# Expert loop: VectorE computes the rest of the U block ahead of the dot products of the fetched rows

## The reference

```python
def expert_block(args):
    hb, eb, gb = args
    a = jnp.einsum('tkd,td->tk', u_tab[eb], hb)
    w = (jax.nn.gelu(a.astype(jnp.float32)) * gb).astype(hb.dtype)
    return jnp.einsum('tk,tkd->td', w, v_tab[eb])
```

## Time and profile before

| | |
|---|---|
| three runs | 5817.51, 5834.57, 5834.54 us |
| median | 5834.54 us |
| the profiled execution | 5836.66 us |
| its span | 5834.9 us |
| TensorE matmuls busy | 4834.1 us (83% of the span) |
| VectorE busy | 4288.8 us (74%) |
| ScalarE busy | 1814.5 us (31%) |
| GpSimd busy | 975.0 us (17%) |
| dot products of fetched rows (L2525) | 448 of 1220 ns |
| additions of fetched rows (L2535) | 448 of 1282 ns |
| rest of a U block (L2495) | 256 of 1220 ns |
| rest of a V block (L2500) | 256 of 1225 ns |
| rounding of a U block (L2448) | 256 of 1047 ns |
| rounding of a V block (L2452) | 256 of 1052 ns |

### The profile page before, as it was taken

One profiled execution on the slowest core, in us unless ns is written; L12 is line 12 of the kernel. 1 busy time (PEld: TensorE's weight loads), 2 busy tenths in 40 slices (PEclk: granted clock), 3 DMA queues, 4 the chain that ended last, 5 costly groups with the idle time before them and its releaser, 6 DMA issues. The chain is left out here.

```text
span 5834.9 us, 69400 instructions
## 1 busy us (share of the span) xinstructions
PE 4834.1 (83%) x23606; PEld 3848.4 (66%) x23606; DVE 4288.8 (74%) x7455; ACT 1814.5 (31%) x3273; POOL 975.0 (17%) x708
## 2 busy tenths in 40 slices
PE   7696738889697869999999778878795669999997
PEld 5385726634575658888888547734674558788886
DVE  1647576767635979999999768658636978888887
ACT  0222311221122753333333221221222743333333
POOL 0000005600000003333333125200000012222221
PEclk9798868999898989999999889989997779999999
DMA  6152317821122569999999548502121369999996
GB/s 226 65 166 76 112 43 265 306 70 61 55 86 94 147 200 352 394 390 385 395 397 396 212 169 311 194 30 93 38 87 36 99 205 342 348 340 342 340 343 230
DMA packets 458724, 1231.49 MB, mean 211 GB/s; under 512 B 210275, under 2 KB 244484, under 8 KB 397382
## 3 DMA queue, kind: packets, MB, share of 16 engines
q1 hardware_dynamic: 357192, 625.56, 30.8%
q0 software_dynamic: 101376, 604.02, 27.3%
HBM read 1169.37 MB, written 60.03 MB: 211 GB/s over the span
## 5 line engine op out<-in xcount | busy, mean ns | idle before, releaser
L2398 POOL DMA_INDIRECT arena<-in_peer_uv,kept x448 | 636.6, 1421 | 3470.6 <-POOLq L2249 1967.2
L233 PE MATMUL psum<-v_ring_hi,w_parts 128*128 128x512 f32 x2560 | 844.4, 394 | 11.5 <-DVE ring_lo L2500 10.9
L233 PE MATMUL psum<-h_hi,u_ring_hi 128*128 128x384 f32 (+1 forms) x2048 | 682.3, 333 | 90.9 <-DVE ring_lo L2495 90.8
L233 PE MATMUL psum<-h_hi,ring_lo 128*128 128x384 f32 (+1 forms) x2048 | 676.3, 330 | 0.0
L233 PE MATMUL psum<-h_lo,u_ring_hi 128*128 128x384 f32 (+1 forms) x2048 | 675.3, 330 | 0.0
L2535 DVE SCALAR_TENSOR_TENSOR arena<-arena 128x1024 f32<-128x1024 f32 x448 | 558.5, 1282 | 19.2
L2525 DVE CUSTOM_DVE_ANT_0 arena<-arena 128x1024 f32<-128x1024 f32 x448 | 536.5, 1220 | 36.9 <-DMA arena<-in_peer_uv,kept 36.4
L233 PEld LDWEIGHTS psum<-v_ring_hi,w_parts 128*128 128x128 f32 x2560 | 480.7, 188 | 120.6 <-DVE ring_lo L2500 17.8
L233 PE MATMUL psum<-ring_lo,w_parts 128*128 128x512 f32 x1280 | 503.0, 393 | 0.0
L233 PEld LDWEIGHTS psum<-h_hi,u_ring_hi 128*128 128x128 f32 x2048 | 395.9, 193 | 134.9 <-DVE ring_lo L2495 67.3
L2500 DVE TENSOR_TENSOR ring_lo<-kept,v_ring_hi 128x1024 fp32r<-128x1024 f32 x256 | 313.7, 1225 | 130.2 <-ACT v_ring_hi L2452 116.2
(11 more groups left out here) (386 smaller groups left out, 9707.4 us busy)
## 6 DMA issues: line engine op xcount, KB each, us to landing
kept<-in_mix SPq DMA_DIRECT2D x312, 512.0 KB
kept<-in_peer_u SPq DMA_DIRECT2D x256, 512.0 KB
kept<-in_peer_uv SPq DMA_DIRECT2D x256, 512.0 KB
kept<-in_ada SPq DMA_DIRECT2D x96, 512.0 KB
gate_scratch<-arena SPq DMA_DIRECT2D x11, 4096.0 KB, 20.8
arena<-gate_scratch SPq DMA_DIRECT2D x64, 384.0 KB
arena<-gate_scratch SPq DMA_DIRECT2D x64, 320.0 KB
spec_scratch<-arena SPq DMA_DIRECT2D x4, 2048.0 KB, 8.5
```

The source lines that it names most:

```text
L233: done = pe.matmul(out, lhs[x], rhs[y], start=first and j == 0, stop=last and j == 2)
L2398: pool.indirect_dma_start(rows[q % NBUF], None, peer_uv, bass.IndirectOffsetOnAxis(ap=at, axis=0))\
```

## The change

VectorE's step computes `rest_u(b, k + 3)` directly behind `weigh(b, k + 1)` and ahead of `dots(b, k)`; before it stood behind the dot products and `rest_w`. Nothing else differs: same instructions, same waits, same buffers, in both layers. The other engines' programs are untouched.

```diff
                     def step(b, k, at):
                         if at_most(b, k, NK - 1):
                             weigh(b, k + 1)
+                        if at_most(b, k, NK - 3):
+                            rest_u(b, k + 3)
                         dots(b, k)
                         if at_most(b, k, NK - 1):
                             rest_w(b, k + 1)
-                        if at_most(b, k, NK - 3):
-                            rest_u(b, k + 3)
                         if at_most(b, k, NK - 1):
                             rest_v(b, k + 1)
                         add_rows(b, k, at)
```

## The result

The changed kernel takes 6358.16 us (median of 4 runs, 6354.39 to 6358.86) against 5834.56 for the kernel before: ratio 1.0901, 95% interval 1.088 to 1.0921. The forecast was 6356. The profiled execution has a span of 6356.0 us, 521 more than before.

A forecast was written before the change was run, and what follows sets the result against it. TensorE, VectorE and DMA were taken as nearly full in layer 0; with both ScalarE waits bare, VectorE's chain sets the new step. 5836.7 + 306 (layer 0) + 213 (layer 1) = 6356 us, range 6260 to 6490.

The forecast's parts named there:

- The U wait: VectorE ahead of rest_u, for ScalarE's rounding: layer 0 start 2.10 us after weigh's start, 1.63 us new idle time.
- The V wait: VectorE ahead of rest_v: it starts 1.68 us after rest_w, which covers only 0.47, so 1.21 us new idle time.
- The step of layer 0: VectorE's step in layer 0's expert loop grows from 8.58 to 11.03 us; over 125 steps, +306 us.
- The step of layer 1: VectorE's layer 1 steps: one-row 8.74 us, two-row 10.87, plus 0.05 each; 1231 us instead of 1017.7, +213.
- The row wait: VectorE's wait for fetched rows, 33.7 us in layer 0 before, goes to zero as the step is longer.
- the load waits of both loops: Waits for U and V loads, layer 1's 1.00 us a step, costed at zero; 125 us if all stayed.
- The DMA share: Layer 0's DMA share falls from 0.99 to about 0.77, as a longer step moves unchanged bytes.
- rival B: TensorE at the low clock becomes the bound: 6766 us with 0.5 of its work slowed, 7770 with all; chance 0.07.
- Rival C: Layer 1's load waits stay on top of the forecast: 6481 us; chance 0.07.
- D: Only one wait shows on VectorE: 6053 us without the V wait, 5948 without the U wait; chance 0.07 together.
- E: ScalarE has U rounded already when VectorE reaches rest_u, so the move is neutral: 5837 us; chance 0.02.
- F: The earlier rest of U ends TensorE's waits for it in layer 1, 69 us: 5768 us; chance 0.01.

The follow-up runs named there:

- e2: Kernel before with rest_v moved ahead of rest_u, both behind the dot products, so only the V wait is bare: 6014.0 us, ratio 1.0311.
- e5: Changed kernel with ScalarE rounding U ahead of w and rest_v moved behind the additions: 5895.8 us, ratio 1.0094 to the kernel before.
- e3: Changed kernel with rest_v moved behind the additions, so only the U wait is bare: 6052.8 us, ratio 1.0375 to the kernel before.
- e12: Kernel before with rest_v moved behind the additions and ScalarE rounding U ahead of w: 5770.3 us, ratio 0.9889.

## Why the prediction was right

It held step by step, most of it within a tenth of a microsecond. Some of the closeness of the total is luck, as said below.

- **The U wait.** From weigh to rest_u 2.10 us was written, 2.09 measured (2705.52 to 2707.61); in layer 1 2.19 was taken from one step, 2.12 is the rule there (5404.60 to 5406.72):

```profile
5404.60 0.48 DVE L2510 TENSOR_TENSOR arena<-arena 128x320 f32<-128x320 f32 x1
5406.72 1.22 DVE L2495 TENSOR_TENSOR ring_lo<-kept,u_ring_hi 128x1024 fp32r<-128x1024 f32 x1 [1.63 <-ACT u_ring_hi L2448]
...
5413.25 0.49 DVE L2510 TENSOR_TENSOR arena<-arena 128x320 f32<-128x320 f32 x1
...
5424.24 0.49 DVE L2510 TENSOR_TENSOR arena<-arena 128x320 f32<-128x320 f32 x1
```

- **The V wait,** which the diff doesn't touch, was the term that is easy to miss. From rest_w to rest_v 1.68 was taken from the last steps of before; 1.73 measured in layer 0, 1.68 in layer 1. e2 shows it alone.
- **The step of layer 0:** 11.03 against 11.04, +306 against +307. The 0.05 us of unexplained stall that the forecast left in makes up for the 0.05 by which the V wait was taken too short; that is luck.
- **The step of layer 1:** +213 against +211, where small errors met. A one-row step takes 8.65 (5404.60 to 5413.25; 8.68 on average), not 8.74. A two-row step takes 10.99 (5413.25 to 5424.24) and not 10.87: I had carried over layer 0's difference, though the shorter weigh and rest_w of layer 1 cover less. The 0.05 added to each has no counterpart.
- **What goes.** The row wait went to zero and the load waits of both loops too, as the 13 and 15.5 us of room had said.
- **The DMA share** was mis-sized: 0.77 written for layer 0, 0.83 measured, though 301 GB/s are just 387 x 8.58 / 11.04. The share does not fall in proportion to the bytes. Nothing hung on it.
- **TensorE's idle time** was taken too long: it is recorded as busy for 8.96 us of a step of layer 0 (1119.62 / 125), not 8.47, with the same number of matmuls, and stands still for 2.1 and not 2.6. Why its busy time grew isn't shown; nothing in the sum hung on it.
- **TensorE's clock** (rival B) cost nothing, though it did fall. In layer 0 it is 1.00, with gaps of 1.41 us ahead of the hidden product and 0.68 ahead of the output product of the step shown, and none above 1.6 once the loop runs. (At its start the clock is 0.50 until 2201.5, behind a gap of 3.77 us.) In layer 1, where the longest gaps are 1.91 and 2.07 us, the mean is 0.96: read in half microseconds, the clock fell to 0.50 thirty times, each time within 2 us after such a gap. 61 gaps were that long, so about half of them had no fall behind them. No step was longer for it: the two-row steps of layer 1 take 10.96 to 11.00 us, all 62 of them, and the 63 one-row steps 8.60 to 8.74. The step is the sum of VectorE's chain, and what the low clock took came out of TensorE's idle time.

```profile
2708.89 0.44 PE L233 MATMUL psum<-h_hi,u_ring_hi 128*128 128x384 f32 x1 [1.41 <-DVE ring_lo L2495]
...
2714.05 0.50 PE L233 MATMUL psum<-v_ring_hi,w_parts 128*128 128x512 f32 x1 [0.68 <-DVE ring_lo L2500]
```

Layer 1, a gap, and a stretch behind it at 1.2 GHz:

```profile
5112.90 0.51 PE L233 MATMUL psum<-h_hi,u_ring_hi 128*128 128x320 f32 x1 [2.06 <-DVE ring_lo L2495]
...
5114.00:5115.00 1.00, 1.00 (x5) 1.00 (x5) 0.32 (x1) 1.00 (x3) 0.00 (x0) 0.50 0.95 336
```

The warning of the Trainium skill cited in the prediction, that such a loop can start every tile at the low rate, was borne out in part: in the running loop of layer 0 no rate was lost, in layer 1 the low rate came after about half of the long gaps. The section's own example waits longer between tiles than this loop ever does, so its full case is not tested here.

Rival C (load waits on top) fell with the changed kernel, but waits for loads returned in e2's layer 1 and above all in e5: as soon as the steps are short again, the early place runs into the U loads. Rivals D, E and F fell by e2, e3 and the result itself.

## What to carry to other kernels

Before an instruction is moved ahead, ask what its producer waits for: if that is the instruction just ahead of the new place, the move bares a round trip, on every pass. Then ask what the moved instruction had covered where it stood; here its going cost 1.2 us a step on a wait that the diff never names. The useful move was the opposite one, to put the instruction with the latest input (rest_v, whose block is loaded and rounded last) behind the longest work that needs nothing from it: one exchange of lines, 1.7% faster. And covering the waits doesn't make an early place free: between e12 and e5, which differ in that place alone, it still costs 126 us.

## What the runs showed of the hardware that I had not expected

- The DMA share and the bytes don't go together: layer 0 ran at 387 GB/s with a share of 0.99, and at 301 GB/s with 0.83, where 0.77 would be in proportion.
- Gaps of TensorE of 1.41 and 0.68 us in an 11 us step left its clock at 1.00 over layer 0's loop once it ran. In layer 1 of the same run, gaps of 1.91 or 2.07 us stood ahead of each of thirty falls to 0.50, and 31 other gaps of these lengths had no fall behind them.
